# Low parts of the weights: one in four by an accumulating DMA, in a two-layer encoder on one core

## The chip, the cores and the metric

One Trainium2 chip, one of its cores. The metric is the device time of one execution in microseconds (us); lower is better.

## The reference

An encoder of two layers over x of 256 tokens by 2048 features, all in float32. The first layer mixes tokens by causal means over windows of 2, 4, 8 and 16, the second by differential attention with 8 heads over a shared K and V; each is followed by an MLP with squared ReLU and 8192 inner features. The parts that matter here:

```python
def sqrelu_mlp(h, w_in, w_out):
    u = jax.nn.relu(h @ w_in)
    return (u * u) @ w_out

for l in range(DEPTH):
    if l < N_A_LAYERS:
        h = h + multiscale_pool_mixer(rms_norm(h, mix_norm[l]), pool_w[l], pool_scale[l])
    else:
        j = l - N_A_LAYERS
        h = h + diff_attention(rms_norm(h, mix_norm[l]), k, v, w_q[j], lam[j], subln[j],
                               w_o[j], cos, sin, l)
    h = h + sqrelu_mlp(rms_norm(h, mlp_norm[l]), w_mlp_in[l], w_mlp_out[l])
    if l == N_A_LAYERS - 1:
        k, v = shared_kv(h, kv_norm, w_kv, cos, sin)
return rms_norm(h, final_norm)
```

## The kernel before

Every product with weights is made of three matmuls in TensorE's float32r format. A weight w is split into w_hi, its value rounded to float32r, and w_lo = w - w_hi; the activations are split likewise. The product is hi x w_hi + hi x w_lo + lo x w_hi (lines 906, 907 and 908).

The weights (some 340 MB, each used once) come in 81 strips of 2048 rows by 512 columns, or of 512 rows by 2048 columns. A strip is cut into HALVES = 8 pieces, here called halves, of 128 partitions x 2 x 512 (512 KB); there are 648. Each goes through these steps:

- SyncE loads it (`load_strip`, line 304) into one of RAW = 4 buffers, half n into `raw[:, n % 4]`, four halves ahead: before it overwrites a buffer it waits on `lo_ready` until the low part of the half that was there is made. Its issues are in order, so a wait for one buffer holds the loads behind it.
- ScalarE writes `w_hi[:, n]` (`split`, line 379). It waits for the load, and for `pe_done` of the same half of the strip before, because w_hi and w_lo hold one strip each.
- VectorE writes `w_lo[:, n]` as raw minus w_hi (`split`, line 588) and signals `lo_ready`.
- TensorE waits for `lo_ready` and makes the 12 matmuls of the half (`group`), then signals `pe_done`.

So while TensorE works at half n of a strip, the other engines prepare the next strip behind it. Between these steps the engines do the rest of the work in an order that is written out by hand: ScalarE the ReLU (line 420), the high parts of the turned activations (406, 413), squares, exponentials (530); VectorE the squaring (628), the addition to the residual stream h (`h_add`, 636), the low parts of activations (608, 614, 621), maxima and differences of the attention; TensorE the transposes (924). GpSimd does only nine small powers (x to the -1/2, lines 359 and 365) after the means of the norms, which VectorE and ScalarE wait for.

The stages: 1 strip of pooling weights, 32 of the first MLP, 8 of K and V, 4 of the queries, 4 of the output product (the attention of four pairs of heads lies beside these eight, in a loop over t), 32 of the second MLP. In an MLP the strips of w_in and w_out alternate; the loop over j turns over two strips, one of each.

Of the kernel before, what the change touches and what calls it, by code (L numbers as in the profile page):

```python
# [23 lines left out]
F32 = mybir.dt.float32  # L24
F32R = mybir.dt.float32r
ACT = mybir.ActivationFunctionType
ALU = mybir.AluOpType
# [9 lines left out]
HALVES = 2 * NG  # L37
RAW = 4
# [3 lines left out]
PAIRS = HEADS // 2  # L42
# [12 lines left out]
S_MLP = (1, 1 + 2 * NJ + 3 * PAIRS + PAIRS)  # L55
S_KV = 1 + 2 * NJ
S_Q = S_KV + 2 * PAIRS
S_O = S_Q + PAIRS
STRIPS = S_MLP[1] + 2 * NJ
# [71 lines left out]
def trunk(nc, x, mix_norm, mlp_norm, pool_w, pool_scale, kv_norm, w_kv, w_q, lam, subln, w_o,  # L131
          w_mlp_in, w_mlp_out, final_norm, keep_consts, pool_consts, out):
    with ExitStack() as ctx:
        def sb(name, shape, dt=F32, scope=ctx):
            return scope.enter_context(nc.sbuf_tensor(name, shape, dt))

        def sem(name):
            return ctx.enter_context(nc.semaphore(name))
# [22 lines left out]
        raw = sb("raw", [P, RAW, 2, SW])  # L161
        w_hi = sb("w_hi", [P, HALVES, 2, SW], F32R)
        w_lo = sb("w_lo", [P, HALVES, 2, SW], F32R)
# [59 lines left out]
        final_landed = sem("final_landed")  # L223
        raw_landed = [sem(f"raw_landed{i}") for i in range(RAW)]
        hi_ready = sem("hi_ready")
        lo_ready = sem("lo_ready")
        pe_done = sem("pe_done")
        t_ready = sem("t_ready")
        t_hi = sem("t_hi")
# [66 lines left out]
        @block.sync  # L296
        def _(sp):
            def load_strip(s, source, first=False):

                for n in range(HALVES):  # L300
                    if not (first and n < RAW):

                        sp.wait_ge(lo_ready, s * HALVES + n - RAW + 1)
                    sp.dma_start(raw[:, n % RAW], source(n // 2, n % 2)).then_inc(raw_landed[n % RAW], 16)

            in_view = w_mlp_in.rearrange("l (c p) n -> l p c n", p=P)
            out_view = w_mlp_out.rearrange("l (c p) n -> l p c n", p=P)
            kv_view = w_kv.rearrange("(c p) n -> p c n", p=P)
            q_view = w_q.rearrange("l (c p) n -> l p c n", p=P)
            o_view = w_o.rearrange("l (c p) n -> l p c n", p=P)  # L310
            pool_view = pool_w.rearrange("l g (c p) n -> l g p c n", p=P)

            def in_rows(view, col):
                return lambda g, hf: view[:, 4 * g + 2 * hf:4 * g + 2 * hf + 2, bass.ds(col, SW)]

            def out_rows(view, j):
                return lambda g, hf: view[:, bass.ds(4 * j + 2 * hf, 2), SW * g:SW * (g + 1)]

            def load_mlp(layer):
                s0 = S_MLP[layer]  # L320
                load_strip(s0, in_rows(in_view[layer], 0))
                load_strip(s0 + 1, in_rows(in_view[layer], SW))
                with nc.sync.Fori(1, NJ - 1) as j:
                    load_strip(s0 + 2 * j, out_rows(out_view[layer], j - 1))
                    load_strip(s0 + 2 * j + 1, in_rows(in_view[layer], (j + 1) * SW))
                load_strip(s0 + 2 * NJ - 2, out_rows(out_view[layer], NJ - 2))
                load_strip(s0 + 2 * NJ - 1, out_rows(out_view[layer], NJ - 1))

            for tb in range(TB):
                sp.dma_start(h[:, tb, :], x[0, tb * P:(tb + 1) * P, :]).then_inc(x_landed[tb], 16)  # L330
            sp.dma_start(keep[:], keep_consts).then_inc(keep_landed, 16)
            sp.dma_start(pool_keep, pool_consts).then_inc(pool_landed, 16)
            load_strip(S_POOL, lambda g, hf: pool_view[0, g][:, 2 * hf:2 * hf + 2, :], first=True)
            load_mlp(0)
            with nc.sync.Fori(0, PAIRS) as j:
                load_strip(S_KV + 2 * j, in_rows(kv_view, j * SW))
                load_strip(S_KV + 2 * j + 1, in_rows(kv_view, j * SW + D))
            with nc.sync.Fori(0, PAIRS) as t:
                load_strip(S_Q + t, in_rows(q_view[0], t * SW))
            with nc.sync.Fori(0, PAIRS) as t:  # L340
                load_strip(S_O + t, out_rows(o_view[0], t))

            sp.wait_ge(o_done, 2 * PAIRS)
            sp.dma_start(final_row, final_norm.partition_broadcast(P)).then_inc(final_landed, 16)
            load_mlp(1)
            for i, (tb, cols) in enumerate(DVE_PIECES):
                sp.wait_ge(result_dve, i + 1)
                sp.dma_start(out[0, tb * P:(tb + 1) * P, cols], result[:, tb, cols]).then_inc(stored, 16)
            sp.wait_ge(stored, 16 * (len(DVE_PIECES) + len(ACT_PIECES)))


        @block.gpsimd
        def _(pool):
            nc.gpsimd.memset(neg_half[:], -0.5).then_inc(half_set, 1)
            pool.wait_ge(half_set, 1)

            def inv_rms(k):
                pool.wait_ge(mean_done, k + 1)
                nc.gpsimd.tensor_tensor(rms[:, k, :], mean[:, k, :], neg_half[:, 0:TB], ALU.pow).then_inc(rms_done, 1)

            for k in range(3):
                inv_rms(k)
            for t in range(PAIRS):
                pool.wait_ge(o_mean_done, t + 1)
                nc.gpsimd.tensor_tensor(o_rms[:, t, :], o_mean[:, t, :], neg_half[:], ALU.pow).then_inc(o_rms_done, 1)
            for k in range(3, 5):
                inv_rms(k)


        @block.scalar  # L370
        def _(act):
            def split(s, g, first=False):

                for n in (2 * g, 2 * g + 1):
                    act.wait_ge(raw_landed[n % RAW], 16 * (2 * s + n // RAW + 1))
                    if not first:

                        act.wait_ge(pe_done, (s - 1) * HALVES + n + 1)
                    nc.scalar.activation(w_hi[:, n], raw[:, n % RAW], ACT.Copy).then_inc(hi_ready, 1)  # L379

            def h_squares(k, n, count):

                act.wait_ge(h_added, count)
                for tb in range(TB):
                    done = 1 + (k - 1) * TB * NG + n * TB + tb
                    if n > 0:
                        act.wait_ge(ssq_done, done - 1)
                    nc.scalar.activation(junk[:, tb] if k > 1 else x_norm[:, tb, n * SW:(n + 1) * SW],  # L388
                                         h[:, tb, n * SW:(n + 1) * SW], ACT.Square,
                                         accum_out=ssq[:, k, tb, n:n + 1]).then_inc(ssq_done, 1)  # L390
# [32 lines left out]
            def mlp(layer):  # L423
                s0, k = S_MLP[layer], 2 * layer

                for g in range(NG):
                    if g == 3:
                        act.wait_ge(rms_done, k + 2)
                        u_relu(0, layer, s0, PAIR[0])
                    split(s0 + 1, g)  # L430
                    if g < 2:
                        h_hi(k, g + 2)
# [39 lines left out]
            for n in range(NG):  # L472
                for tb in range(TB):
                    cols = slice(n * SW, (n + 1) * SW)
                    nc.scalar.activation(x_norm[:, tb, cols], h[:, tb, cols], ACT.Copy,
                                         scale=rms[:, 0, tb:tb + 1]).then_inc(x_normed, 1)
# [57 lines left out]
            for t in range(2 * PAIRS):  # L534
                s = S_Q + t
# [47 lines left out]
        def _(dve):  # L583
            def split(s, g):

                for n in (2 * g, 2 * g + 1):
                    dve.wait_ge(hi_ready, s * HALVES + n + 1)
                    nc.vector.tensor_tensor(w_lo[:, n], raw[:, n % RAW], w_hi[:, n].bitcast(F32), ALU.subtract).then_inc(lo_ready, 1)  # L588

            def norm_mean(k):  # L590

# [47 lines left out]
            def mlp(layer):  # L639
# [8 lines left out]
                for g in range(NG):  # L648
                    if g == 3:

                        u_square(1, layer, X)
                    split(s0 + 2, g)
                    if g == 1:
                        u_lo(0, layer, U_FIRST)
# [182 lines left out]
            for t in range(2 * PAIRS):  # L837
                s = S_Q + t
# [53 lines left out]
        def _(pe):  # L892
            ident = keep[:, C_IDENT:C_IDENT + P]

            def group(s, g, tiles, banks, start, stop):

                for hf in range(2):
                    n = 2 * g + hf
                    pe.wait_ge(lo_ready, s * HALVES + n + 1)
                    for kk in range(2):  # L900
                        hi, lo = tiles[2 * hf + kk]
                        begin = start and hf == 0 and kk == 0
                        end = stop and hf == 1 and kk == 1
                        for tb in range(TB):
                            tok = slice(tb * P, (tb + 1) * P)
                            nc.tensor.matmul(banks[tb][:], hi[:, tok], w_hi[:, n, kk, :], start=begin, stop=False)  # L906
                            nc.tensor.matmul(banks[tb][:], hi[:, tok], w_lo[:, n, kk, :], start=False, stop=False)  # L907
                            last = nc.tensor.matmul(banks[tb][:], lo[:, tok], w_hi[:, n, kk, :], start=False, stop=end)  # L908
                    last.then_inc(pe_done, 1)
# [178 lines left out]
            for t in range(2 * PAIRS):  # L1088
                s = S_Q + t
# [37 lines left out]
```

## Time and profile before

| | us |
|---|---|
| median of the two timed executions | 1887.5 |
| the two times | 1886.83, 1888.17 |
| span of the profiled execution, first to last instruction | 1886.5 |
| the profiled execution's own time | not listed apart from the two times, which lie 0.3 to 1.7 above the span |
| TensorE busy | 1851.7 |
| VectorE busy | 1151.0 |
| ScalarE busy | 840.5 |
| GpSimd busy | 10.5 |
| loads moved, GB/s over the span | 185 |

In the rows PE is TensorE's matmul side, PEld its loading of the stationary operand, DVE VectorE, ACT ScalarE, POOL GpSimd, and SPq the queue of SyncE. A row "A <- B: us, times" of the waits is the idle time of A that B ended. Matmuls are pipelined, so the mean of one (390 ns) is longer than the distance between two starts.

### The profile page before, as it was taken

To read this page: it belongs to the slowest core of one execution; us is meant where nothing else is said; L and a number is where in the kernel's file an instruction comes from. 1 tells how busy PE (TensorE), PEld (TensorE's weight loads), DVE (VectorE), ACT (ScalarE), POOL (GpSimd) and SP (SyncE) were. 2 spreads that over 40 slices of the span, in tenths; PEclk is the share of its full clock that TensorE was granted. 3 is DMA by queue.
4 is the path that set the end of the run, shared out by engine and by line. 5 is a ranking of instruction groups with operands and counts; after the bars stand their busy time and mean duration, and the time that the engine had idled before them with its cause. 6 is when DMAs were issued, how large, how long until landed. Compare 5 with 4: busy or idle time off the path is not lost.

```text
span 1886.5 us, 24435 instructions
## 1 busy us (share of the span) xinstructions
PE 1851.7 (98%) x8425; PEld 1539.2 (82%) x8425; DVE 1151.0 (61%) x1417; ACT 840.5 (45%) x1061; POOL 10.5 (1%) x14
## 2 busy tenths in 40 slices
PE   6999999999999999999999999999999999999997
PEld 5788888888888888888888888888888888888886
DVE  6755556665656565755556777565655565556665
ACT  5544444444444444744435545444444444444442
POOL 0000000000000000000000000000000000000000
PEclk9999999999999999999999999999999999999999
DMA  7555555556565655556654446556566555555552
GB/s 263 184 191 184 189 188 178 191 190 197 180 198 181 194 185 192 161 191 196 195 192 149 139 153 212 181 182 193 185 194 193 191 189 187 189 189 178 184 194 89
DMA packets 178009, 348.69 MB, mean 185 GB/s; under 512 B 10594, under 2 KB 10676, under 8 KB 177332
## 3 DMA queue, kind: packets, MB, share of 16 engines
q1 hardware_dynamic: 177408, 346.33, 57.2%
q10 hardware_dynamic: 564, 1.88, 0.3%
q8 instruction: 22, 0.36, 0.1%
q14 instruction: 15, 0.12, 0.0%
HBM read 346.07 MB, written 2.10 MB: 185 GB/s over the span
## 4 chain that ended last, share of the span: by engine, by line
PE 57%; issue 38%; DVE 3%; ACT 1%; DMA 1%; POOL 0%; SPq 0%; POOLq 0%; DVEq 0%
PE bank L908 18%; PE bank L906 18%; PE bank L907 18%; PE bank L924 2%; DVE w_lo L588 1%; DMA raw<-in_pool_w 1%; DVE h L636 0%; DVE a_lo L614 0%; PE bank L1045 0%; ACT w_hi L379 0%; DVE h L730 0%; DVE scratch L727 0%; DVE scratch L702 0%; DVE b_lo L608 0%; PE bank L1061 0%
## 5 line engine op out<-in xcount | busy, mean ns | idle before, releaser
L379 ACT ACTIVATE w_hi<-raw 128x1024 fp32r<-128x1024 f32 x648 | 677.5, 1061 | 809.7 <-PE bank L908 806.6
L588 DVE TENSOR_TENSOR w_lo<-raw,w_hi 128x1024 fp32r<-128x1024 f32 x648 | 774.2, 1220 | 317.0 <-ACT w_hi L379 312.7
L906 PE MATMUL bank<-w_hi,a_hi 128*128 128x512 f32 x1344 | 528.3, 393 | 0.0
L908 PE MATMUL bank<-w_hi,a_lo 128*128 128x512 f32 x1344 | 524.0, 390 | 0.0
L907 PE MATMUL bank<-w_lo,a_hi 128*128 128x512 f32 x1344 | 523.7, 390 | 0.0
L906 PE MATMUL bank<-w_hi,b_hi 128*128 128x512 f32 x1248 | 488.4, 391 | 0.7 <-issue 0.7
L908 PE MATMUL bank<-w_hi,b_lo 128*128 128x512 f32 x1248 | 485.9, 389 | 0.0
L907 PE MATMUL bank<-w_lo,b_hi 128*128 128x512 f32 x1248 | 485.8, 389 | 0.0
L636 DVE TENSOR_TENSOR h<-bank,h 128x512 f32<-128x512 f32 x288 | 185.5, 686 | 230.4 <-PE bank L908 230.4
L908 PEld LDWEIGHTS bank<-w_hi,a_lo 128*128 128x128 f32 x1344 | 252.6, 188 | 52.8
L907 PEld LDWEIGHTS bank<-w_lo,a_hi 128*128 128x128 f32 x1344 | 252.9, 188 | 51.1
L906 PEld LDWEIGHTS bank<-w_hi,a_hi 128*128 128x128 f32 x1344 | 252.8, 188 | 50.9
L906 PEld LDWEIGHTS bank<-w_hi,b_hi 128*128 128x128 f32 x1248 | 234.6, 188 | 49.1 <-issue 0.9
L908 PEld LDWEIGHTS bank<-w_hi,b_lo 128*128 128x128 f32 x1248 | 234.4, 188 | 48.9
L907 PEld LDWEIGHTS bank<-w_lo,b_hi 128*128 128x128 f32 x1248 | 234.5, 188 | 48.3
L628 DVE SCALAR_TENSOR_TENSOR scratch<-bank,rms,scratch 128x512 f32<-128x512 f32 x64 | 45.1, 746 | 123.1 <-ACT scratch L420 123.1
L420 ACT ACTIVATE scratch<-bank,rms 128x512 f32<-128x512 f32 x64 | 40.6, 685 | 140.1 <-PE bank L908 140.1
L924 PEld LDWEIGHTS bank<-keep,scratch 128*128 128x128 f32 x352 | 41.0, 140 | 5.7
L924 PE MATMUL bank<-keep,scratch 128*128 128x128 f32 x352 | 45.5, 272 | 0.0
L621 DVE TENSOR_TENSOR b_lo<-bank,b_hi 128x512 fp32r<-128x512 f32 x64 | 41.0, 682 | 0.0
L413 ACT ACTIVATE b_hi<-bank 128x512 fp32r<-128x512 f32 x64 | 34.2, 586 | 0.0
L388 ACT ACTIVATE scratch<-h 128x512 f32<-128x512 f32 x32 | 19.9, 624 | 26.2 <-DVE h L636 20.5
(81 smaller groups left out, 349.9 us busy)
## 6 DMA issues: line engine op xcount, KB each, us to landing
raw<-in_w_mlp_in SPq DMA_DIRECT2D x256, 512.0 KB, 3.8
raw<-in_w_mlp_out SPq DMA_DIRECT2D x256, 512.0 KB, 4.9
raw<-in_w_kv SPq DMA_DIRECT2D x64, 512.0 KB, 4.1
raw<-in_w_q SPq DMA_DIRECT2D x32, 512.0 KB, 4.9
raw<-in_w_o SPq DMA_DIRECT2D x32, 512.0 KB, 4.2
raw<-in_pool_w SPq DMA_DIRECT2D x8, 512.0 KB, 9.1
h<-in_x SPq DMA_DIRECT2D x2, 1024.0 KB, 6.3
out<-scratch SPq DMA_DIRECT2D x3, 512.0 KB, 4.7
```

Of the source, the lines that this page charges most:

```text
L379: nc.scalar.activation(w_hi[:, n], raw[:, n % RAW], ACT.Copy).then_inc(hi_ready, 1)
L388: nc.scalar.activation(junk[:, tb] if k > 1 else x_norm[:, tb, n * SW:(n + 1) * SW], h[:, tb, n * SW:(n + 1) * SW], ACT.Square, accum_out= ...
L413: nc.scalar.activation(b_hi[:, at + 2 * b:at + 2 * b + 2, :], T[b][:].rearrange("p (c t) -> p c t", c=2), ACT.Copy).then_inc(t_hi, 1)
L420: nc.scalar.activation(relu[:, tb], banks[tb][:], ACT.Relu, scale=rms[:, 2 * layer + 1, tb:tb + 1]).then_inc(relu_done, 1)
L588: nc.vector.tensor_tensor(w_lo[:, n], raw[:, n % RAW], w_hi[:, n].bitcast(F32), ALU.subtract).then_inc(lo_ready, 1)
L621: nc.vector.tensor_tensor(b_lo[:, tiles, :], T[b][:].rearrange("p (c t) -> p c t", c=2), b_hi[:, tiles, :].bitcast(F32), ALU.subtract).the ...
L628: nc.vector.scalar_tensor_tensor(hidden[:, tb], banks[tb][:], rms[:, 2 * layer + 1, tb:tb + 1], relu[:, tb], ALU.mult, ALU.mult).then_inc( ...
L636: last = nc.vector.tensor_tensor(h[:, tb, cols], PAIR[g % 2][tb][:], h[:, tb, cols], ALU.add)
L906: nc.tensor.matmul(banks[tb][:], hi[:, tok], w_hi[:, n, kk, :], start=begin, stop=False)
L907: nc.tensor.matmul(banks[tb][:], hi[:, tok], w_lo[:, n, kk, :], start=False, stop=False)
L908: last = nc.tensor.matmul(banks[tb][:], lo[:, tok], w_hi[:, n, kk, :], start=False, stop=end)
L924: last = nc.tensor.transpose(T[b][:, at:at + P], source(tb, c), ident)
```

## The change

The low parts of halves 3 and 7 of each strip (n % RAW = RAW - 1), one in four, are made in another way. ScalarE writes, right behind w_hi, the same raw half times -1 into w_lo, rounded to float32r as w_hi is. GpSimd waits for it (`minus_hi`) and issues a DMA that adds the raw half onto w_lo, from SBUF to SBUF. TensorE, and SyncE ahead of the refill of raw buffer 3, wait for that DMA (`lo_dma`, 16 for each), and for the other halves on VectorE's `lo_dve`. GpSimd's powers are set in among its DMAs.

```diff
--- before.py
+++ after.py
@@ -223,7 +223,9 @@
         final_landed = sem("final_landed")
         raw_landed = [sem(f"raw_landed{i}") for i in range(RAW)]
         hi_ready = sem("hi_ready")
-        lo_ready = sem("lo_ready")
+        lo_dve = sem("lo_dve")
+        lo_dma = sem("lo_dma")
+        minus_hi = sem("minus_hi")
         pe_done = sem("pe_done")
         t_ready = sem("t_ready")
         t_hi = sem("t_hi")
@@ -300,7 +302,10 @@
                 for n in range(HALVES):
                     if not (first and n < RAW):
 
-                        sp.wait_ge(lo_ready, s * HALVES + n - RAW + 1)
+                        if n % RAW == RAW - 1:
+                            sp.wait_ge(lo_dma, (s * 2 + n // RAW) * 16)
+                        else:
+                            sp.wait_ge(lo_dve, s * 6 + (n // RAW - 1) * 3 + n % RAW + 1)
                     sp.dma_start(raw[:, n % RAW], source(n // 2, n % 2)).then_inc(raw_landed[n % RAW], 16)
 
             in_view = w_mlp_in.rearrange("l (c p) n -> l p c n", p=P)
@@ -358,13 +363,32 @@
                 pool.wait_ge(mean_done, k + 1)
                 nc.gpsimd.tensor_tensor(rms[:, k, :], mean[:, k, :], neg_half[:, 0:TB], ALU.pow).then_inc(rms_done, 1)
 
-            for k in range(3):
-                inv_rms(k)
+            def low(s):
+
+                for n in (RAW - 1, 2 * RAW - 1):
+                    pool.wait_ge(minus_hi, s * 2 + n // RAW + 1)
+                    pool.dma_start(w_lo[:, n], raw[:, n % RAW], accum_op=ALU.add).then_inc(lo_dma, 16)
+
+            inv_rms(0)
+            low(0)
+            low(1)
+            inv_rms(1)
+            for s in range(2, S_KV):
+                low(s)
+            low(S_KV)
+            inv_rms(2)
+            for s in range(S_KV + 1, S_Q + 3):
+                low(s)
             for t in range(PAIRS):
+                low(S_Q + t + 3)
                 pool.wait_ge(o_mean_done, t + 1)
                 nc.gpsimd.tensor_tensor(o_rms[:, t, :], o_mean[:, t, :], neg_half[:], ALU.pow).then_inc(o_rms_done, 1)
-            for k in range(3, 5):
-                inv_rms(k)
+            low(S_Q + PAIRS + 3)
+            low(S_MLP[1])
+            inv_rms(3)
+            for s in range(S_MLP[1] + 1, STRIPS):
+                low(s)
+            inv_rms(4)
 
 
         @block.scalar
@@ -377,6 +401,8 @@
 
                         act.wait_ge(pe_done, (s - 1) * HALVES + n + 1)
                     nc.scalar.activation(w_hi[:, n], raw[:, n % RAW], ACT.Copy).then_inc(hi_ready, 1)
+                    if n % RAW == RAW - 1:
+                        nc.scalar.activation(w_lo[:, n], raw[:, n % RAW], ACT.Copy, scale=-1.0).then_inc(minus_hi, 1)
 
             def h_squares(k, n, count):
 
@@ -584,8 +610,10 @@
             def split(s, g):
 
                 for n in (2 * g, 2 * g + 1):
+                    if n % RAW == RAW - 1:
+                        continue
                     dve.wait_ge(hi_ready, s * HALVES + n + 1)
-                    nc.vector.tensor_tensor(w_lo[:, n], raw[:, n % RAW], w_hi[:, n].bitcast(F32), ALU.subtract).then_inc(lo_ready, 1)
+                    nc.vector.tensor_tensor(w_lo[:, n], raw[:, n % RAW], w_hi[:, n].bitcast(F32), ALU.subtract).then_inc(lo_dve, 1)
 
             def norm_mean(k):
 
@@ -896,7 +924,10 @@
 
                 for hf in range(2):
                     n = 2 * g + hf
-                    pe.wait_ge(lo_ready, s * HALVES + n + 1)
+                    if n % RAW == RAW - 1:
+                        pe.wait_ge(lo_dma, (s * 2 + n // RAW + 1) * 16)
+                    else:
+                        pe.wait_ge(lo_dve, s * 6 + n // RAW * 3 + n % RAW + 1)
                     for kk in range(2):
                         hi, lo = tiles[2 * hf + kk]
                         begin = start and hf == 0 and kk == 0
```

## Rows read from the trace of the kernel before

**Rows 1.** The page's first part: busy us of each engine, share, instructions.

```profile
PE 1851.7 (98%) x8425; PEld 1539.2 (82%) x8425; DVE 1151.0 (61%) x1417; ACT 840.5 (45%) x1061; POOL 10.5 (1%) x14
```

**Rows 2.** Waits: engine, line, waited for, us in total, times, longest.

```profile
ACT w_hi L379 <- PE bank L908: 806.6, 494, 4.3
...
DVE w_lo L588 <- ACT w_hi L379: 312.7, 245, 6.5
...
ACT probs L530 <- DVE row_bias L813: 21.5, 8, 3.1
...
PE bank L977 <- DMA keep<-keep_consts: 9.9, 1, 9.9
...
PE bank L991 <- DMA scratch<-pool_consts: 5.0, 1, 5.0
DVE scratch L874 <- POOL o_rms L365: 4.5, 4, 1.1
...
SPq L304 <- DVE w_lo L588: 1450.2, 644, 14.0
```

**Rows 3.** Busy us by stretch: length, PE, PEld, DVE, ACT, POOL; clock, DMA share, GB/s.

```profile
491.00:537.00 46.00, 46.00 (x213) 38.29 (x212) 26.98 (x29) 19.64 (x21) 0.00 (x0) 1.00 0.58 190
...
1073.00:1100.00 27.00, 25.28 (x119) 20.95 (x118) 21.96 (x53) 13.45 (x35) 1.01 (x1) 1.00 0.40 127
```

**Rows 4.** Chain of work: start us, us, what; one turn of the MLP loop from first to second.

```profile
491.80 0.87 PE bank L924 x8
536.21 0.87 PE bank L924 x8
```

**Rows 5.** Timeline of ScalarE in the MLP: start us, us, engine, line, operation.

```profile
495.45 1.06 ACT L379 ACTIVATE w_hi<-raw 128x1024 fp32r<-128x1024 f32 x1 [1.58 <-PE bank L908]
498.17 1.06 ACT L379 ACTIVATE w_hi<-raw 128x1024 fp32r<-128x1024 f32 x1 [1.66 <-PE bank L908]
...
504.76 2.95 ACT L379 ACTIVATE w_hi<-raw 128x1024 fp32r<-128x1024 f32 x3
```

**Rows 6.** Timeline of VectorE and of SyncE's queue in the same stretch.

```profile
490.21 1.23 DVE L588 TENSOR_TENSOR w_lo<-raw,w_hi 128x1024 fp32r<-128x1024 f32 x1 [1.50 <-ACT w_hi L379]
...
491.60 3.09 SPq L304 DMA_DIRECT2D raw<-in_w_mlp_out  x2
```

**Rows 7.** Busy time by stretch at the start, 50 to 60 us.

```profile
50.00:55.00 5.00, 2.95 (x16) 2.21 (x14) 5.00 (x9) 3.57 (x10) 0.00 (x0) 1.00 0.70 232
55.00:60.00 5.00, 4.93 (x19) 3.78 (x18) 5.00 (x8) 3.45 (x9) 0.00 (x0) 0.66 0.47 159
```

**Rows 8.** The raw tiles from 491 to 537 us: issues, times to landing.

```profile
L304 SPq DMA_DIRECT2D raw<-in_w_mlp_in x8: 372/373/373, 497.9 to 518.2; - x8
...
DMA to landing us min/median/max: 3.5/4.0/5.7
```

**Rows 9.** DMA issues: tile, queue, count, KB each, median us to landing.

```profile
raw<-in_w_mlp_in SPq DMA_DIRECT2D x256, 512.0 KB, 3.8
raw<-in_w_mlp_out SPq DMA_DIRECT2D x256, 512.0 KB, 4.9
...
h<-in_x SPq DMA_DIRECT2D x2, 1024.0 KB, 6.3
...
scratch<-in_final_norm SPq DMA_DIRECT2D x1, 1024.0 KB, 7.0
```

**Rows 10.** DMA queues: packets, MB, share of 16 engines.

```profile
q1 hardware_dynamic: 177408, 346.33, 57.2%
```

**Rows 11.** Timeline at the first ring turn and at the end.

```profile
22.79 1.99 ACT L379 ACTIVATE w_hi<-raw 128x1024 fp32r<-128x1024 f32 x2
...
23.87 2.36 DVE L588 TENSOR_TENSOR w_lo<-raw,w_hi 128x1024 fp32r<-128x1024 f32 x2 [0.43 <-ACT w_hi L379]
...
1854.39 2.35 DVE L588 TENSOR_TENSOR w_lo<-raw,w_hi 128x1024 fp32r<-128x1024 f32 x2
...
1874.52 0.39 PE L908 MATMUL bank<-w_hi,b_lo 128*128 128x512 f32 x1
```

## The prediction

> **What bounds the kernel now.** I read the page's shares first: TensorE is busy for 98% of the span, VectorE 61%, ScalarE 45%, GpSimd 1% [rows 1]. A busy TensorE may still be badly fed, so the waits come next: TensorE's two longest waits for others are 9.9 and 5.0 us for the first constants, while ScalarE waited 806.6 us for TensorE and SyncE 1450.2 us for VectorE's low parts [rows 2]. A stretch in the middle of the MLP confirms it: 46.00 us of 46.00 busy at a granted clock of 1.00 [rows 3]. One turn of the MLP loop (two strips, 16 half-groups) takes 536.21 - 491.80 = 44.4 us [rows 4], so four half-groups, one turn of the ring of raw buffers, take 11.1 us. Any work taken from VectorE there is worth nothing.
>
> How far ahead do the weights run? ScalarE writes w_hi of half n of the next strip as soon as TensorE has finished half n of this one; its rows show one write of 1.06 us every 2.72 us, each after a wait for TensorE [rows 5]. TensorE reads it seven halves later, 7 x 2.72 = 19 us. So a low part a few us late hurts nobody once. What can hurt is a rate: everything that a raw buffer goes through must fit into a ring turn.
>
> **The change, part by part.**
>
> Removed: 162 of the 648 subtractions on VectorE, 1.22 us each alone [rows 6]: 198 us off an engine that waits for ScalarE 312.7 us already [rows 2]. Worth 0 in the steady part; TensorE hides it. At the start VectorE is the engine that is full (5.00 us of 5 from 50 to 55 us, [rows 7]), and four subtractions of 1.14 us go there, at most 4.6 us, if the DMA that replaces them isn't later.
>
> Added on ScalarE: 162 copies of the same shape as w_hi. A back-to-back one costs (2.95 - 1.06) / 2 = 0.95 us [rows 5]: 154 us, share 45% to 53%. Hidden, as ScalarE waits for TensorE. Without cover (the attention stage, eight strips, two copies each) it is 16 x 0.95 = 15 us.
>
> Added on GpSimd: 162 DMA issues on an engine that is idle 99%. Behind them queue the nine power operations; VectorE now waits 4.5 us in all for the four of the attention [rows 2]. An issue of a DMA takes 0.37 us on SyncE [rows 8]; GpSimd's isn't shown. With 0.37 to 2 us each, nine times, that is 3 to 18 us where nothing covers it; I take 5, and only in the rival below.
>
> Moved: the wait of SyncE. The refill of raw buffer 3 now waits for the DMA, and the refills of buffers 0, 1 and 2 stand behind it in SyncE's order. Buffer 3's turn now is: hand-off from the end of a low part to SyncE's issue, 491.60 - (490.21 + 1.23) = 0.16 us [rows 5, 6]; load to landing, 4.35 us (256 loads of the MLPs at 3.8 and 256 at 4.9, [rows 9]; these are 512 of the 648); w_hi 1.06; subtraction 1.22. Sum 6.8 us of 11.1, so ScalarE finds its raw data landed and waits for TensorE only. After the change: 0.16 + 4.35 + 1.06 + 0.95 + X = 6.52 + X, X being the time from GpSimd's release to the landing of the accumulating DMA.
>
> So X decides. No such DMA is in the trace. From below: a load of the same 512 KB from SyncE lands in 3.5 us at best, 4.0 in the middle [rows 8]. That has one read and one write per element; the accumulate reads two streams of 512 KB and writes one. Nearest rows for that many bytes read: the 1024 KB loads, 6.3 us (x) and 7.0 us (final norm) [rows 9]. From above: 7.0 plus one load's data in between on the same DMA engines (57.2% of 1886.5 us over 660 loads, 1.6 us, [rows 10]) = 8.6 us. I take 6.3, the faster of the two rows with its number of bytes, since both sides of the copy are in the core. The ends 3.5 and 8.6 are kept.
>
> The Trainium skill, "DMA: Bandwidth & Descriptors", section "Anatomy of one DMA", speaks against my value: it gives a GpSimd-issued DMA about 2.0 us plus its bytes over 436 GB/s. As an estimate from that page X would be 3.2 us, the turn 9.7 us, and the time unchanged; no run here shows it, and the formula is for a plain copy. Its result is the first rival.
>
> The sum: if the turn of buffer 3 is longer than TensorE's, it sets the rate of everything, 162 turns with 161 between first and last. Before, the first low part of half 3 ends at 23.87 + 2.36 = 26.2 us and that of the last half at 1854.39 + 2.35 = 1856.7 us [rows 11]: 11.37 us a turn. After: w_hi of half 3 ends at 22.79 + 1.99 = 24.8 [rows 11], the negated copy at 25.7, the DMA at 25.7 + X. Then 161 x (6.52 + X). Then TensorE, with no queue left, does the last half (2.72) and the end runs as now: last matmul over at 1874.52 + 0.39 = 1874.9, so 11.6 us more [rows 11]. In all 40.0 + X + 161 x (6.52 + X). With X = 6.3: 46.3 + 161 x 12.82 = 2110 us of span. The span before is 1886.5 and the two times are 1886.8 and 1888.2, so 1 us lies around it: 2111 us, 12% slower. Equal to the time before where X = 4.92; 2% slower from X = 5.2.
>
> What is late next once this turn rules: TensorE idles 12.8 - 10.9 = 1.9 us per turn, probably in one piece. At the start of the kernel it idled 2.05 us of the 5 from 50 to 55 us and its granted clock was 0.66 in the next 5 [rows 7]. A stretch like that, part of it at 1.2 instead of 2.4 GHz, loses 5 x (1 - 0.66) = 1.7 us; one in each turn makes TensorE's turn 12.6 us, which the turn of 12.8 still covers. I count nothing for it.
>
> **The rivals.**
>
> 1. The DMA is hidden, not slower. X is between 3.5 and 4.9 us, place: the turn of raw buffer 3, which then takes 10.0 to 11.4 us, under TensorE's 11.4; the deciding point is X = 4.92. For it: the load of equal size lands in 3.5 to 4.0, the DMA engines are 58% busy in the MLP [rows 3], TensorE is 19 us behind. Against it: double reads, and descriptors made by GpSimd. Time 1887.5 - 4.6 at the start, if the DMA isn't late there, to 1890: I take 1886.
>
> 2. ScalarE or GpSimd becomes late where in-order work already touches TensorE. In the attention TensorE is busy only 25.28 of 27 us [rows 3] and ScalarE waits for VectorE's row_bias 21.5 us [rows 2]. Price 15 + 5 us as above: 1907 us, within 2%. Against it: ScalarE is busy only half of that stretch, 13.45 of 27 us [rows 3].
>
> 3. The accumulating DMA is slower than any row bounds, X above 8.6 us: the sum gives 2483 us at 8.6 and 162 us more for each further us. For it: a word-by-word add inside a DMA and software descriptors, which no row shows. Against it: nothing but the size of the 1024 KB rows.
>
> 4. It doesn't do what it says: GpSimd's in-order DMA issue stalls the chain (a power operation ahead of a DMA waits for a mean that needs it). The order in the code puts each power operation behind the strips that its mean needs, so I give it nothing beyond rival 2.
>
> **How the numbers follow.** Buffer 3's turn rules with X from 4.9 to 8.6: 0.60. Hidden: 0.26. ScalarE or GpSimd late by some 20 us: 0.05. X above 8.6: 0.08. A gain of over 2% has 0.01: TensorE's 1851.7 busy us would have to shrink. Range: from 1880 (hidden, with all of the start's gain) to 2480 (X = 8.6). It leaves out some 0.1 to 0.15. The forecast's own range is 1890 to 2480. Two per cent is about what a measurement of this kernel can tell from no change; the forecast's low corner from 4.92 to 5.2 falls within it and takes 0.04 from the slower side: faster 0.01, same 0.35, slower 0.64.
>
> **What would show it.** Right: ScalarE's w_hi waits for the DMA into raw, not for TensorE; SyncE's longest waits are for the accumulating DMA; TensorE waits at the low parts; its busy share falls to some 88%; the starts of w_hi of halves 3 and 7 lie about 12.8 us apart; VectorE is some 190 us less busy, ScalarE some 155 more. Hidden (rival 1): ScalarE still waits 500 us or more for TensorE and the accumulating DMA lands within 4.9 us of the negated copy. Rival 2: TensorE's new idle time lies between 1000 and 1160 us alone. Rival 3: landing times above 8.6 us. Wrong in another way: landing under 4.9 us and TensorE yet idle throughout, or landing over 6 us and the time unchanged, which would mean that the refill isn't bound to the DMA as I read it.

## The result, and the profile after

The changed kernel takes 1949.3 us (1948.9 to 1949.6), the kernel before 1887.5: a ratio of 1.033, 95% interval 1.031 to 1.034. It is slower, as forecast, but by 62 us and not by 224.

First the page of the changed kernel: busy times, its queues and DMA issues.

```profile
span 1947.5 us, 24473 instructions
...
PE 1868.0 (96%) x8425; PEld 1542.3 (79%) x8425; DVE 963.2 (49%) x1255; ACT 981.0 (50%) x1223; POOL 150.9 (8%) x176
...
q1 hardware_dynamic: 177408, 346.33, 53.5%
q0 software_dynamic: 23328, 84.95, 22.8%
...
raw<-in_w_mlp_in SPq DMA_DIRECT2D x256, 512.0 KB, 5.4
raw<-in_w_mlp_out SPq DMA_DIRECT2D x256, 512.0 KB, 6.0
w_lo<-raw POOLq DMA_DIRECT2D x162, 512.0 KB, 5.0
```

Against [rows 1] VectorE does 188 us less, ScalarE 140 more, GpSimd 140 more, and none of that is the loss. TensorE's idle time grew from 34.8 to 79.5 us (span less busy time), 44.7 us, and its busy time by 16.3 us: together the 61.0 us by which the span grew. Part of the added busy time is a lower granted clock: before, it stood at 1.00 in the MLP [rows 3]; now it is below that in some stretches, 0.97 from 150 to 200 us, as the busy times by stretch show (columns as in [rows 3]). Over the whole span the mean fell from 0.996 to 0.992, which is worth 0.008 x 1947.5 - 0.004 x 1886.5 = 8 us of full speed, half of the 16.3. For the rest there is only an estimate: the matmul ahead of a gap is shown with its whole 0.39 us, where another start follows after 0.23 without a gap, and the trace has 42 unbroken stretches of matmuls instead of 10, which makes 5 us.

```profile
150.00:200.00 50.00, 47.64 (x208) 39.07 (x207) 24.51 (x28) 23.70 (x26) 3.44 (x4) 0.97 0.72 213
```

The waits show who holds whom (columns as in [rows 2]):

```profile
ACT w_hi L403 <- DMA raw<-in_w_mlp_out: 349.5, 153, 6.6
ACT w_hi L403 <- DMA raw<-in_w_mlp_in: 320.5, 130, 6.5
DVE b_lo L649 <- ACT b_hi L439: 219.7, 32, 7.8
...
ACT w_hi L403 <- PE bank L939: 96.8, 52, 6.0
...
PE bank L937 <- DVE b_lo L649: 30.4, 23, 3.3
...
SPq L309 <- DMA w_lo<-raw: 1376.9, 161, 10.5
SPq L309 <- DVE w_lo L616: 132.7, 49, 14.0
```

ScalarE waited 806.6 us for TensorE before; now it waits 96.8 us for TensorE and 670 us for the MLP's loads. SyncE, which issues these, waits 161 times for the accumulating DMA. The weights no longer run ahead of TensorE. The loss lies where most of the strips are: from w_hi of half 3 in a stage's first strip to the same point in the next stage, the first MLP took 746.3 us instead of 714.9 and the second one, up to its last strip, 714.6 instead of 691.6, together 54 of the 61 us.

The chain of waits from 528 to 550 us is one turn of raw buffer 3 after another (start us, us, what):

```profile
524.08 3.84 DMA raw<-in_w_mlp_out
...
528.91 1.05 ACT w_lo L405
529.96 0.28 issue
530.25 5.10 DMA w_lo<-raw
...
535.52 3.98 DMA raw<-in_w_mlp_in
...
539.60 0.08 ACT w_hi L403
539.68 0.88 issue
540.57 1.05 ACT w_lo L405
541.62 0.28 issue
541.90 4.52 DMA w_lo<-raw
...
546.58 3.74 DMA raw<-in_w_mlp_in
```

Load 3.98, w_hi 0.96 (0.08 + 0.88), negated copy 1.05, hand-off 0.28, DMA 4.52 to 5.10, SyncE 0.17: 11.1 and 11.4 us here, from load to load. Over the whole kernel it is more. By the rows of the tile w_lo (issue time min/median/max in ns, first and last start in us) the 162 DMAs are issued from 25.9 to 1922.3 us, 1896.4 / 161 = 11.78 us a turn, against 11.37 before. Both are means over all stages, the attention too, where turns are longer.

```profile
L370 POOL DMA_DIRECT2D w_lo<-raw x162: 859/862/1035, 25.9 to 1922.3; - x162
...
DMA to landing us min/median/max: 4.5/5.0/8.2
```

### The profile page after: what moved, and what is told of

It reads as the page before. It is cut to its first block, busy times and chain, and to the rows that moved or that the text cites. A ratio compares the mean times of both kernels' runs of the same rounds, so it can differ in the third digit from the quotient of the medians.

```text
span 1947.5 us, 24473 instructions
## 1 busy us (share of the span) xinstructions
PE 1868.0 (96%) x8425; PEld 1542.3 (79%) x8425; DVE 963.2 (49%) x1255; ACT 981.0 (50%) x1223; POOL 150.9 (8%) x176
## 4 chain that ended last, share of the span: by engine, by line
DMA 61%; PE 16%; issue 10%; ACT 10%; DVE 1%; SPq 1%; ACTq 0%; POOL 0%; DVEq 0%; POOLq 0%
DMA w_lo<-raw 34%; DMA raw<-in_w_mlp_out 12%; DMA raw<-in_w_mlp_in 10%; ACT w_lo L405 7%; PE bank L937 5%; PE bank L938 5%; PE bank L939 5%; DMA raw<-in_w_kv 2%; ACT w_hi L403 1%; DMA raw<-in_w_q 1%; DMA raw<-in_pool_w 1%; PE bank L955 1%; DMA raw<-in_w_o 1%; SPq L309 0%; PE bank L1076 0%
## 5 line engine op out<-in xcount | busy, mean ns | idle before, releaser
L616 DVE TENSOR_TENSOR w_lo<-raw,w_hi 128x1024 fp32r<-128x1024 f32 x486 | 587.2, 1221 | 559.4 <-ACT w_hi L403 545.8
L937 PE MATMUL bank<-w_hi,b_hi 128*128 128x512 f32 x1248 | 493.7, 396 | 35.2 <-DVE b_lo L649 30.4
L370 POOL DMA_DIRECT2D w_lo<-raw x162 | 140.2, 865 | 1748.2 <-ACT w_lo L405 1715.1
L405 ACT ACTIVATE w_lo<-raw 128x1024 fp32r<-128x1024 f32 x162 | 168.9, 1043 | 0.0
L649 DVE TENSOR_TENSOR b_lo<-bank,b_hi 128x512 fp32r<-128x512 f32 x64 | 41.2, 686 | 219.7 <-ACT b_hi L439 219.7
```

The source lines that it names most:

```text
L370: pool.dma_start(w_lo[:, n], raw[:, n % RAW], accum_op=ALU.add).then_inc(lo_dma, 16)
L405: nc.scalar.activation(w_lo[:, n], raw[:, n % RAW], ACT.Copy, scale=-1.0).then_inc(minus_hi, 1)
L649: nc.vector.tensor_tensor(b_lo[:, tiles, :], T[b][:].rearrange("p (c t) -> p c t", c=2), b_hi[:, tiles, :].bitcast(F32), ALU.subtract).the ...
```

## The experiments

Three theories went in. A: the turn of raw buffer 3 sets the rate. B: the DMA's traffic slows the loads (their landing went from 3.8 and 4.9 to 5.4 and 6.0 us). C: ScalarE's 162 added copies cost the time.

**The copy first, w_hi beside the DMA (e1_swap).** TensorE and SyncE wait for w_hi as well; for that SyncE's loops are written out.

```diff
+                    if n % RAW == RAW - 1:
+                        nc.scalar.activation(w_lo[:, n], raw[:, n % RAW], ACT.Copy, scale=-1.0).then_inc(minus_hi, 1)
                     nc.scalar.activation(w_hi[:, n], raw[:, n % RAW], ACT.Copy).then_inc(hi_ready, 1)
-                    if n % RAW == RAW - 1:
-                        nc.scalar.activation(w_lo[:, n], raw[:, n % RAW], ACT.Copy, scale=-1.0).then_inc(minus_hi, 1)
```

> Theory A, the turn of raw buffer 3 (load 3.9 us, w_hi 1.0, negated copy 1.05, hand-off 0.28, accumulating DMA 5.0, SyncE 0.2: 11.4 to 11.75 us a turn) sets the rate. ScalarE now writes the negated copy first and w_hi beside the DMA, which takes 1.0 us out of the turn and nothing else out of the kernel: 10.4 to 10.8 us, under TensorE's 11.37. Expected 1885 to 1900 us. Rival B, the DMA's traffic slows the loads (landing 5.4 and 6.0 us instead of 3.8 and 4.9): the traffic is the same, so about 1949. Rival C, ScalarE's 162 added copies cost the time: they are all still there, so about 1949.

Measured: 1892.8 us, ratio 1.0026 (1.0017 to 1.0036). The edit gives back 56 of the 62 us, with all of B's bytes and C's copies in place. It is not the swap alone: with SyncE's loops written out, the step from the DMA's landing to SyncE's next load fell from 0.14 to 0.02 us in the mean, 0.12 x 161 = 19 us of turns. Both shorten the turn of buffer 3, so theory A stands, but how the 56 us divide between the two isn't shown. The page's DMA issues have the loads landing in 5.0 and 6.2 us, about as late as in the changed kernel (5.4 and 6.0), so late landings by themselves cost nothing.

```profile
raw<-in_w_mlp_in SPq DMA_DIRECT2D x256, 512.0 KB, 5.0
raw<-in_w_mlp_out SPq DMA_DIRECT2D x256, 512.0 KB, 6.2
w_lo<-raw POOLq DMA_DIRECT2D x162, 512.0 KB, 5.5
```

The late loads of the changed kernel are those of buffers 0 to 2. SyncE, held by buffer 3, issues all four within 2.2 us:

```profile
512.46 2.24 SPq L309 DMA_DIRECT2D raw<-in_w_mlp_out  x4
```

These four landed in 4.3, 5.9, 6.5 and 7.3 us. The load of buffer 3, the only one in the turn, took 3.97 us in the mean of the changed kernel and 4.56 in the kernel before: it got faster, against theory B.

In e1, the rows of the tile w_lo give the first and the last issue:

```profile
L371 POOL DMA_DIRECT2D w_lo<-raw x162: 859/859/1035, 24.9 to 1865.0; - x162
```

The turn is (1865.0 - 24.9) / 161 = 11.43 us, close to TensorE's own 11.37. The DMA now lands in 5.5 us instead of 5.0, which takes back half of what the swap gave. So the turn of buffer 3 is hardly shorter than TensorE's: the accumulating DMA still has 12.6% of the chain that ended last (33.8% in the changed kernel).

**The DMA for half 7 only (e2_only7).**

```diff
-                    if n % RAW == RAW - 1:
+                    if n in (7,):
```

> Only half 7 of each strip is made by the DMA (81 instead of 162), half 3 by VectorE again. Theory A, with turns that the 19 us between ScalarE and TensorE can average: one turn of 11.7 and one of about 7 us fit into TensorE's 22.7, so nothing is left of the loss: 1885 to 1892 us. Rivals B and C, a cost for each DMA or each copy: half of the 62 us stays, about 1918.

Measured: 1886.9 us, ratio 0.9997 (0.9987 to 1.0006): the loss is gone, not halved. One long turn (its DMA lands in 5.8 us) and one short one average out. It is a rate that costs, no single delay.

**The DMA reads the weights from HBM (e3_hbm).** Buffer 3 is free after the negated copy.

```diff
-                    pool.dma_start(w_lo[:, n], raw[:, n % RAW], accum_op=ALU.add).then_inc(lo_dma, 16)
+                    pool.dma_start(w_lo[:, n], source(s, n), accum_op=ALU.add).then_inc(lo_dma[n], 16)
...
-                            sp.wait_ge(lo_dma, (s * 2 + n // RAW) * 16)
+                            sp.wait_ge(minus_hi, s * 2 + n // RAW)
```

> The DMA adds the piece of the weights from HBM instead of raw buffer 3, and SyncE refills the buffer as soon as the negated copy is made. Theory A: the DMA is out of the turn, which is about 6.3 us; TensorE waits for the low part 19 us later and doesn't see it: 1885 to 1892 us. Rival B: the bytes moved are the same and 85 MB more come from HBM, so the loads are slowed as before or more: 1949 or above. Rival C: 1949, as the copies stay.

Measured: 1883.8 us, ratio 0.9979 (0.9969 to 0.9988), the lowest of all runs. Its DMA is slower than any other, and its loads land as late as in the changed kernel, by the page's DMA issues:

```profile
raw<-in_w_mlp_in SPq DMA_DIRECT2D x256, 512.0 KB, 5.4
raw<-in_w_mlp_out SPq DMA_DIRECT2D x256, 512.0 KB, 5.7
w_lo<-in_w_mlp_in POOLq DMA_DIRECT2D x64, 512.0 KB, 8.9
w_lo<-in_w_mlp_out POOLq DMA_DIRECT2D x64, 512.0 KB, 8.2
```

Over all of them the rows of the tile give the median:

```profile
DMA to landing us min/median/max: 5.6/8.5/11.8
```

But SyncE's waits name VectorE and ScalarE, not the DMA:

```profile
SPq L319 <- DVE w_lo L653: 1319.3, 483, 13.9
SPq L319 <- ACT w_lo L442: 110.9, 49, 5.3
```

And TensorE is full in the MLP (busy times by stretch):

```profile
60.00:500.00 440.00, 440.00 (x1987) 365.25 (x1986) 216.95 (x239) 224.31 (x245) 48.30 (x40) 1.00 0.85 236
```

A DMA of 8.5 us outside the turn costs nothing; one of 5.0 us inside it costs 62 us. TensorE is busy for 440.00 of 440 us while the DMA engines are 85% busy, against 77% in the changed kernel from 60 to 500 us. As the cause of the 62 us theory B is out.

**ScalarE's copies without the DMA (e4_copy)**, on the kernel before:

```diff
                     nc.scalar.activation(w_hi[:, n], raw[:, n % RAW], ACT.Copy).then_inc(hi_ready, 1)
+                    if n % RAW == RAW - 1:
+                        nc.scalar.activation(w_lo[:, n], raw[:, n % RAW], ACT.Copy, scale=-1.0).then_inc(minus_hi, 1)
```

> The kernel before, with ScalarE's negated copies of halves 3 and 7 into w_lo added, and VectorE's subtraction over them as before; no DMA. Theory A: buffer 3's turn becomes 4.35 + 2.0 + 1.2 + 0.2 = 7.8 us, hidden: 1885 to 1892 us. Rival C, ScalarE's work costs: up to 1949. Rival B has nothing to add here: 1887.

Measured: 1890.9 us, ratio 1.0015 (1.0005 to 1.0025). The copies alone cost about 3 us of the 62.

**Four DMAs a strip (e5_four)**, for halves 1, 3, 5 and 7, a semaphore each:

```diff
-                    if n % RAW == RAW - 1:
+                    if n in (1, 3, 5, 7):
```

> Halves 1, 3, 5 and 7 are made by the DMA (324), each with a semaphore of its own. Theory A: buffers 1 and 3 both have a turn of 11.7 us, side by side; ScalarE's two more copies of 1 us and the DMAs' meeting on the same engines lengthen it to 12 to 13 us: 1990 to 2150 us. Rival B, a cost per byte moved: the loss doubles, about 2011, and the share of the DMA engines rises to 95% or more. Rival C, a cost per copy: 2011 too, with ScalarE's waits for the loads gone.

Measured: 2103.8 us, ratio 1.114 (1.111 to 1.118). Twice the DMAs cost 3.5 times as much, 216 us, so it is no fixed price per DMA, byte or copy. One turn of it on the chain of waits:

```profile
536.25 5.10 DMA raw<-in_w_mlp_in
...
542.41 1.05 ACT w_lo L412
543.46 0.28 issue
543.74 4.55 DMA w_lo<-raw
...
548.44 4.89 DMA raw<-in_w_mlp_out
```

The accumulating DMA is as fast as before (median 5.0), but the load in the turn takes 4.9 to 5.1 us instead of 3.8 to 4.0, and the DMA engines are 95% busy (next to last column):

```profile
500.00:600.00 100.00, 92.94 (x410) 76.32 (x409) 34.93 (x40) 50.86 (x56) 13.79 (x16) 0.98 0.95 254
```

Here traffic does enter, through the turn; the 95% are what rival B had said. This turn is 548.44 - 536.25 = 12.2 us. In the mean it is longer, by the rows of the tile w_lo, which run from the first half 1 to the last half 7, 161.5 turns: (2076.9 - 20.3) / 161.5 = 12.73 us.

```profile
L377 POOL DMA_DIRECT2D w_lo<-raw x324: 862/862/1035, 20.3 to 2076.9; - x162
```

TensorE's granted clock falls to a mean of 0.961, but that isn't what lengthens the turn of buffer 3: its load takes 5.19 us in the mean instead of 3.97, and w_hi starts 0.19 us after the landing.

**A plain copy in place of the add (e6_plain).** w_lo, a float32r tile as before, becomes the whole weight.

```diff
-                    pool.dma_start(w_lo[:, n], raw[:, n % RAW], accum_op=ALU.add).then_inc(lo_dma, 16)
+                    pool.dma_start(w_lo[:, n], raw[:, n % RAW]).then_inc(lo_dma, 16)
```

> The DMA copies the raw half over w_lo instead of adding it, so w_lo is the whole weight and not its low part. It measures what the adding costs inside the DMA. If the second stream that is read is what makes 5.0 us (my forecast took 6.3 for two streams), the landing falls to 3.5 to 4.0 us, the turn to 10.7 and the time to 1885 to 1900. If the time is made of fixed steps and of GpSimd's descriptors (0.86 us each), it stays at 4.7 to 5.0 and the time at 1935 to 1949.

**Half of the bytes (e7_half).** Only the first 512-column piece is added; the other stays the negated weight.

```diff
-                    pool.dma_start(w_lo[:, n], raw[:, n % RAW], accum_op=ALU.add).then_inc(lo_dma, 16)
+                    pool.dma_start(w_lo[:, n, 0:1], raw[:, n % RAW, 0:1], accum_op=ALU.add).then_inc(lo_dma, 16)
```

> The DMA adds only the first of the two 512-column pieces (256 KB instead of 512), so half of w_lo stays the negated weight. If the 5.0 us are mostly moved bytes, the landing falls by 1.0 to 1.5 us and with a turn of 10.5 us the time is 1885 to 1900. If they are mostly fixed, it falls by less than 0.5 and the time stays above 1915.

Measured: 1885.9 us (ratio 0.9991, 0.998 to 1.0002) and 1885.1 us (0.9983, 0.9972 to 0.9994); both hide the DMA. The issues and landings of the plain copy, then of the half:

```profile
L370 POOL DMA_DIRECT2D w_lo<-raw x162: 530/530/695, 25.9 to 1856.5; - x162
...
DMA to landing us min/median/max: 2.9/4.3/6.7
```

```profile
L370 POOL DMA_DIRECT2D w_lo<-raw x162: 859/859/1032, 25.8 to 1855.0; - x162
...
DMA to landing us min/median/max: 3.3/4.2/6.9
```

The medians may not be comparable: where TensorE rules, the DMA probably meets loads at other moments (not shown). I compare the shortest landings: plain 2.9 us, half an add 3.3, a whole add 4.5. From these two adds, half the bytes cost 1.2 us, so as an estimate 512 KB cost 2.4 and 2.1 us are fixed, GpSimd's 0.86 us of issuing among them; the plain copy lands the same 512 KB in 1.6 us less than the add, 0.33 of it in the issue.

**Three quarters of the bytes (e8_threequarters)**, columns 0 to 383 of each piece.

```diff
-                    pool.dma_start(w_lo[:, n], raw[:, n % RAW], accum_op=ALU.add).then_inc(lo_dma, 16)
+                    pool.dma_start(w_lo[:, n, :, 0:384], raw[:, n % RAW, :, 0:384], accum_op=ALU.add).then_inc(lo_dma, 16)
```

> The DMA adds 384 of each 512 columns (384 KB in pieces of 1.5 KB); the other low parts stay the negated weight. Theory A in numbers: the whole DMA lands in 5.0 us with a turn of 11.78, at least 4.5; the half in 3.3 at least. Three quarters land in some 4.3 to 4.6, which makes the turn 11.1 to 11.4, just under TensorE's 11.37: 1885 to 1900 us. If the price followed the bytes moved beside the loads (rival B), three quarters of the loss of 62 us would stay: 1934.

Measured: 1900.7 us, ratio 1.007 (1.0053 to 1.0087), a little above A's range and far from B's 1934. The rows of its tile w_lo:

```profile
L370 POOL DMA_DIRECT2D w_lo<-raw x162: 1200/1200/1356, 25.9 to 1872.1; - x162
...
DMA to landing us min/median/max: 4.4/4.5/7.3
```

The turn is (1872.1 - 25.9) / 161 = 11.47 us. The shortest landing fell by 0.1 us only: with rows cut in two pieces GpSimd needs 1.20 us to issue instead of 0.86. By the estimate above 384 KB would land in 3.9 us, with 0.34 more for the issue in 4.2; 0.2 us stay unexplained.

**Two DMAs of 256 KB (e9_two)**, both waited for.

```diff
-                    pool.dma_start(w_lo[:, n], raw[:, n % RAW], accum_op=ALU.add).then_inc(lo_dma[n], 16)
+                    for kk in range(2):
+                        pool.dma_start(w_lo[:, n, kk], raw[:, n % RAW, kk], accum_op=ALU.add).then_inc(lo_dma[n], 16)
```

> The same 512 KB are added by two DMAs of 256 KB, issued one after the other by GpSimd, and TensorE and SyncE wait for both. The bytes, the copies and the result are as in the changed kernel. Theory A: the second issue (0.86 us) lengthens the turn by 0.4 to 0.9 us, 161 times: 2015 to 2095 us. Rivals B and C: nothing that they count has changed, 1949. If two DMAs in flight overlap so well that the last lands no later, 1949 as well, with a landing of both within 5.0 us of the first issue.

Measured: 1981.6 us, ratio 1.050 (1.048 to 1.051). It got slower with nothing of B's or C's changed, but by 32 us and not by the 66 to 146 of theory A, whose range is missed. It is no price per DMA either: e5 has as many DMAs and lost 216 us, e9 94. On the chain the second DMA starts 0.54 us after the first and lands in 4.3 us instead of 5.0:

```profile
535.98 0.54 POOL w_lo L378
536.52 4.32 DMA w_lo<-raw
```

From the first issue to the last, less that 0.54, the turn is (1954.3 - 25.8 - 0.54) / 161 = 11.97 us, by the rows of the tile w_lo:

```profile
L378 POOL DMA_DIRECT2D w_lo<-raw x324: 859/926/1241, 25.8 to 1954.3; - x162
```

That is 0.19 us longer than in the changed kernel. (161 x 0.19 = 31 us is the difference of the spans told once more and proves nothing by itself.) What grew is seen in the parts of the turn, from the times of every turn in each run's trace:

| means over 161 turns of buffer 3, us | changed kernel | e1 | e6 | e8 | e9 | e5 |
|---|---|---|---|---|---|---|
| DMA, issue to (last) landing | 5.12 | 5.58 | 4.44 | 4.75 | 5.28 | 4.89 |
| to SyncE's load | 0.14 | 0.02 | 0.14 | 0.14 | 0.15 | 0.14 |
| load to landing | 3.97 | 4.10 | 3.97 | 3.99 | 4.03 | 5.19 |
| landing to ScalarE's start | 0.23 | 0.36 | 0.51 | 0.26 | 0.19 | 0.19 |
| ScalarE inside the turn | 2.00 | 1.06 | 2.00 | 2.00 | 2.00 | 2.00 |
| hand-off to GpSimd | 0.31 | 0.31 | 0.31 | 0.32 | 0.32 | 0.32 |
| turn | 11.78 | 11.43 | 11.37 | 11.47 | 11.97 | 12.73 |

The fourth row holds every wait for TensorE, at whatever clock, and for ScalarE's other work; its median in the changed kernel is 0.10 us. In e9 the two DMAs together take 0.16 us longer and the load 0.06. In e6 the turn is TensorE's 11.37, and the transfers leave room for waits of 0.5 us.

## Why the prediction was right in direction and wrong in size

- **The bound, and what the removed work is worth.** Right. VectorE lost 188 us (198 forecast) and it bought nothing in the steady part, where TensorE was full before (440.00 of 440 us) and is full in e3.
- **The turn of raw buffer 3 as the new bound.** Right, and shown: with 1.1 us less of other steps in the turn (e1) 56 of the 62 us go, with the DMA out of it (e3) all of them, copies and bytes moved staying in place; with a long turn only every second time (e2) nothing is lost.
- **"I take 6.3".** This is the step that failed: the DMA takes 5.0 us in the middle and 5.12 in the mean, so X, with the hand-off from ScalarE, was 5.43. I took the 6.3 us of a 1024 KB load from HBM for its number of bytes read. 0.87 us too much in each of 161 turns are 140 of the 162 us by which 2111 was too high. The shortest landings give 4.5 us for the add, as an estimate 2.1 fixed and 2.4 for the 512 KB. The Trainium skill, "DMA: Bandwidth & Descriptors", section "Anatomy of one DMA", gives a DMA issued by GpSimd about 2.0 us plus its bytes over 436 GB/s, as an estimate 3.2 us for 512 KB, and names no price for adding. The plain copy of e6 agrees, with 2.9 at the least and 4.3 in the middle; the add lies 1.3 us above the formula at the least. By the formula alone the loss would have been missed altogether.
- **"Load to landing, 4.35 us".** Too long by some 0.4: in the turn the load takes 3.97 us in the mean, as the first of its burst. Against it stand 0.23 us between landing and w_hi, which I had put at nothing; so the parts other than X are 6.35 us instead of 6.52, in part by luck.
- **The sum.** The form held. The loss is 161 times a difference of two nearly equal numbers: 12.82 - 11.37 forecast, 11.78 - 11.37 measured. An error of 9% in the turn became one of 3.6 times in the loss. With the measured turn my sum gives 25.7 + 5.3 + 161 x 11.78 + 14.3 = 1941.9 us; the span is 1947.5. As the turn is measured, this tests only the two ends. The rest lies at the last one: I had TensorE one half behind the last DMA, 2.7 us. The last DMA is issued at 1922.3 and with 5.0 us lands at 1927.3, but matmuls still start until 1935.4 us.
- **"TensorE waits at the low parts".** Wrong in place. Its longest wait for others is 30.4 us for VectorE's b_lo at the start of w_out's strips. ScalarE turns the hidden activations into b_hi behind its split of half 3 of the very same strip (`u_hi` after g = 1), and the load of half 3 is the one that is issued late, so by the order of the code the lateness reaches TensorE through the activations before it does through the weights. VectorE waits 219.7 us for b_hi.
- **The clock, counted as nothing.** Small, but not shown to be nothing. I had expected a low stretch in each turn; the granted clock was 1.00 in most stretches of the MLP and 0.992 over the span, 8 us of full speed less than before. In the turn it can only show between landing and w_hi. That is 0.23 us in the mean and 0.10 in the median turn, so the clock and all other waits there account, as an estimate, for no more than 0.13 x 161 = 21 us.
- **Rival 1 (hidden).** Not this kernel, which missed it by 0.41 us a turn; e2, e6 and e7 are hidden, and e1 and e8 nearly. The deciding point X = 4.92 was well placed: e6 is hidden at a mean X of 4.75, e8 loses 13 us at 5.07.
- **Rival 2 (ScalarE or GpSimd late).** e4 puts the copies at 3 us; in the changed kernel TensorE is busy for 194.47 us of the 200 from 1000 to 1200 us, the attention, where it was 198.27: 1.9% less, and in the second MLP (1200 to 1860 us) 644.91 where it was 660.00, 2.3% less. The attention is no special place.
- **Rival 3 (above 8.6 us).** Not here: the longest landing is 8.2 us. From HBM (e3) the same add took 8.5 us in the middle.

What stays open: why e3 gains 3.8 us. Its trace shows where. TensorE is busy 41.45 us of the first 60, at a granted clock of 1.00, against 39.97 at 0.94 in the kernel before, and for 199.83 of the 200 us from 1000 to 1200 against 198.27: 3 us in two places where TensorE had idled in the kernel before. That VectorE's relief did it is likely, but wasn't tried alone.

## What to carry to other kernels

When a step that frees a ring buffer is moved to a slower path, sum the buffer's whole turn (refill, every use, hand-offs) and compare it with the ring's period at the bounding engine; slack ahead of the consumer doesn't help against a rate. Where the two are within 10%, the forecast is a coin between nothing and a loss on every turn, so state it so, and look first at what needn't be inside the turn: here, one copy moved out of it and SyncE's loops written out, 1.1 us of 11.8, were worth 56 us. Add up means and not medians, as a rate is made of means. A slow transfer belongs where it holds no buffer that others need.

## What I had not expected of the hardware

- An accumulating DMA of 512 KB within SBUF lands in 4.5 us at best, with 223 GB/s moved in all over the span; a plain one in 2.9. GpSimd's issue takes 0.86 us for the add, 0.53 for the copy, and 1.20 for an add in pieces of 1.5 KB or from HBM.
- An add from HBM landed in 8.5 us in the middle (5.6 at best) against 5.0, and TensorE was still fully busy with the DMA engines at 85%.
- Two adds of half the size, one behind the other, finished 0.54 + 4.3 = 4.9 us after the first issue in the turn shown, but 5.28 in the mean of all, against 5.12 for one DMA with all the bytes.
